# Branch A's key stack in other memory and its first stacks ahead of the last index scores; rotary products and index relu in PSUM

## The reference

```python
def partial_rope(x, cos, sin):
    x1 = xf[..., :half]
    x2 = xf[..., half:ROT_DIM]
    return concatenate([x1 * c - x2 * s, x2 * c + x1 * s, xf[..., ROT_DIM:]], axis=-1)

logits = einsum('bqhd,bsd->bqhs', iqb, ik)
score = einsum('bqhs,bqh->bqs', relu(logits), iwb)
score = where(admissible[None], score, -inf)
_, sel = top_k(score, n_sel)                      # n_sel = 128
s = einsum('bqhgd,bqnhd->bhgqn', qg, k_sel) * scale
p = softmax(s); o = einsum('bhgqn,bqnhd->bqhgd', p, v_sel)
```

## Time and profile before

| | us |
|---|---|
| median of 3 runs | 1347.4 |
| lowest, highest | 1344.56, 1348.52 |
| the profiled execution, whole | 1349.22 |
| its span in the trace | 1347.4 |
| PE busy in it | 1296.7 (96%) |
| DVE, ACT, POOL busy | 721.9 (54%), 622.9 (46%), 617.9 (46%) |
| mean granted TensorE clock | 0.984 of full |

### The profile page before, as it was taken

How to read it: one execution, slowest core, us unless ns; L and a number is a source line. 1 busy time by engine, 2 the same in 40 slices (tenths; PEclk the granted TensorE clock), 3 DMA queues, 4 the chain that set the end, 5 groups by cost and what they waited for, 6 DMA issues and landing times.

```text
span 1347.4 us, 19944 instructions
## 1 busy us (share of the span) xinstructions
PE 1296.7 (96%) x6525; PEld 1087.5 (81%) x6525; DVE 721.9 (54%) x1444; ACT 622.9 (46%) x1119; POOL 617.9 (46%) x767
## 2 busy tenths in 40 slices
PE   5999899999999999999999989999999999999997
PEld 3788788888887888888878868888888878888876
DVE  5688987865446212112658997778545532121154
ACT  4445555776544333323244356576754433233332
POOL 3555433433234545555765543334222445555472
PEclk8999899999999999999999989999999999999998
DMA  5322211221132233233142222112213222332321
GB/s 181 134 92 94 79 63 47 63 87 55 48 110 71 86 101 94 87 105 112 65 175 91 94 81 76 48 55 78 73 48 110 79 71 86 103 99 86 101 94 62
DMA packets 37030, 117.39 MB, mean 87 GB/s; under 512 B 4064, under 2 KB 6496, under 8 KB 36448
## 3 DMA queue, kind: packets, MB, share of 16 engines
q1 hardware_dynamic: 34368, 111.37, 24.9%
q10 hardware_dynamic: 2592, 5.11, 1.3%
HBM read 110.18 MB, written 6.29 MB: 86 GB/s over the span
## 4 chain that ended last, share of the span: by engine, by line
PE 84%; DVE 7%; ACT 4%; issue 2%; POOL 1%; DMA 0%; ACTq 0%; DVEq 0%; SPq 0%; POOLq 0%
PE acc L592 68%; PE ps_o L705 4%; PE ps_t L692 3%; PE ps_s L662 1%; PE ps_t L683 1%; PE ps_o L712 1%; PE ps_s L668 1%; DVE att_c L1311 1%; POOL w_lo L541 1%; PE ps_s L651 1%; DVE ak_s L1152 1%; PE spare L644 1%; DVE score L1179 1%; ACT prob L937 1%; PE ps_s L676 1%
## 5 line engine op out<-in xcount | busy, mean ns | idle before, releaser
L541 POOL TENSOR_TENSOR w_lo<-w_raw,w_hi 128x256 fp32r<-128x256 f32 x752 | 606.5, 837 | 697.2 <-ACT w_hi L787 697.2
L592 PE MATMUL acc<-h_hi,w_hi 128*128 128x512 f32 x1136 | 457.3, 403 | 0.4 <-ACT w_hi L787 0.4
L592 PE MATMUL acc<-h_lo,w_hi 128*128 128x512 f32 x1136 | 448.1, 394 | 0.0
L592 PE MATMUL acc<-h_hi,w_lo 128*128 128x512 f32 x1136 | 297.4, 396 | 2.1 <-POOL w_lo L541 2.1
L787 ACT ACTIVATE w_hi<-w_raw 128x1024 fp32r<-128x1024 f32 (+1 forms) x212 | 203.9, 962 | 130.8 <-PE acc L592 100.6
L592 PEld LDWEIGHTS acc<-h_hi,w_hi 128*128 128x128 f32 x1136 | 215.7, 190 | 41.7 <-ACT w_hi L787 1.3
L592 PEld LDWEIGHTS acc<-h_lo,w_hi 128*128 128x128 f32 x1136 | 215.6, 190 | 40.0
L592 PEld LDWEIGHTS acc<-h_hi,w_lo 128*128 128x128 f32 x1136 | 208.5, 188 | 43.3 <-POOL w_lo L541 3.0
L1324 DVE SCALAR_TENSOR_TENSOR gated<-prob,acc 128x512 f32<-128x512 f32 x16 | 11.0, 687 | 247.6 <-PE acc L592 247.6
L987 ACT ACTIVATE prob<-acc,par_half 128x512 f32<-128x512 f32 x48 | 33.1, 690 | 148.3 <-PE acc L592 148.3
L937 ACT ACTIVATE prob<-prob,neg_max 128x128 f32<-128x128 f32 (+3 forms) x128 | 70.6, 552 | 32.6 <-DVE neg_max L1214 32.0
(11 more groups left out here) (239 smaller groups left out, 1837.1 us busy)
## 6 DMA issues: line engine op xcount, KB each, us to landing
w_raw<-w_full SPq DMA_DIRECT2D x164, 512.0 KB, 3.4
w_raw<-w_mix SPq DMA_DIRECT2D x48, 256.0 KB, 2.6
x_kept<-xT SPq DMA_DIRECT2D x2, 2048.0 KB, 9.4
rel<-rel ACTq DMA_DIRECT2D x16, 256.0 KB, 2.7
xT<-x_kept SPq DMA_DIRECT2D x2, 2048.0 KB, 9.6
stage<-x SPq DMA_DIRECT2D x4, 512.0 KB, 7.0
out<-stage SPq DMA_DIRECT2D x4, 512.0 KB, 2.6
consts<-consts ACTq DMA_DIRECT2D x1, 640.0 KB, 4.2
```

The source lines that it names most:

```text
L541: last = pool.tensor_tensor(w_lo[:, slot, part, :], w_raw[:, raw, part, :], w_hi[:, slot, part, :].bitcast(F32), ALU.subtract)
L592: last = pe.matmul(acc[slot][:, :], w[:, slot, k, :], x[:, k, :], start=(i == 0), stop=(i == 3 * nk - 1))
```

## The change

Four edits.

1. `ak_s` moves from `r0` to the start of `r3`, where branch C's values `cv` will be written much later. The two slots of `aq_s` are swapped: n uses slot (n + 1) % 2, so that n = 0 no longer lies on `ik_s`; the wait for the last index product moves from `ak_hi` to `aq_hi 1`. Branch B's first stacks move by two rows within `r0` to follow the slots.
2. `ak_hi`, `ak_lo` with `aq_hi`, and `aq_lo` of item block 0 go with units 10, 14 and 15. `index (3, h)` goes one unit later (unit 17). `ROUNDS` gives 2 rounds to units 8 to 13 and 4 to units 14 to 16: 24 before the items, 26 in the kernel before. The other two come in the items, so that the mask for t = 3 is written after item 23 instead of item 21.
3. In `rope` the product with the sines goes to PSUM, to the bank `ps_o`, and the last addition reads it there.
4. In `index` ACT writes the relu to PSUM, to `ps_t[h % 2]`, and DVE reads it there.

```diff
-INDEX_AT = {11: 2, 15: 3}
+INDEX_AT = {U_AK + 7: 2, U_AK + 12: 3}
+STACKS_A = {5: ("ak_hi",), 9: ("ak_lo", "aq_hi"), 10: ("aq_lo",)}
-ROUNDS = {8: 2, 9: 2, 10: 2, 11: 2, 12: 2, 13: 4, 14: 4, 15: 4, 16: 4}
+ROUNDS = {U_AK + n: 2 if n < 10 else 4 for n in range(4, 13)}
...
-        if u == 15:
-            seq.extend((("ak_hi", 0), ("aq_hi", 0)))
-        if u == 16:
-            seq.extend((("ak_lo", 0), ("aq_lo", 0)))
+        for step in STACKS_A.get(u - U_AK, ()):
+            seq.append((step, 0))
...
-        ak_s = at("ak_s", [P, 2, 2, SEQ], F32R, r0)
-        bq_s = [at("bq_s0", [P, SEQ], F32R, r0 + 4 * ROW), at("bq_s1", [P, SEQ], F32R, r0)]
+        bq_s = [at("bq_s0", [P, SEQ], F32R, r0 + 6 * ROW), at("bq_s1", [P, SEQ], F32R, r0)]
...
         cv = at("cv", [P, NT, CH, P + 1], F32, r3)
+        ak_s = at("ak_s", [P, 2, 2, SEQ], F32R, r3)
...
-                        act.wait_ge(score_full, l * SCORE_USES + SCORE_USE[("index", (NT - 1, IDX_HEADS - 1))] + 1)
...
                     elif kind == "aq_hi":
                         act.wait_ge(roped, l * ROPES + ROPES)
+                        if n == 1:
+                            act.wait_ge(score_full, l * SCORE_USES + SCORE_USE[("index", (NT - 1, IDX_HEADS - 1))] + 1)
...
-                        act.activation(prob[:, h % 2, 0:(t + 1) * P], ps_s[use % 2][:, 0:(t + 1) * P], ACT.Relu)\
+                        act.activation(ps_t[h % 2][:, 0:(t + 1) * P], ps_s[use % 2][:, 0:(t + 1) * P], ACT.Relu)\
...
-                        link(dve.tensor_tensor(turn[:, :], turn[:, :], sin, ALU.mult))
+                        link(dve.tensor_tensor(ps_o[:, :], turn[:, :], sin, ALU.mult))
                         link(dve.tensor_tensor(t, t, cos, ALU.mult))
-                        dve.tensor_tensor(t, t, turn[:, :], ALU.add).then_inc(roped, 1)
+                        dve.tensor_tensor(t, t, ps_o[:, :], ALU.add).then_inc(roped, 1)
...
-                            dve.tensor_scalar(dst, prob[:, h % 2, 0:w], iw[:, t, h:h + 1], None, ALU.mult).then_inc(score_part, 1)
+                            dve.tensor_scalar(dst, ps_t[h % 2][:, 0:w], iw[:, t, h:h + 1], None, ALU.mult).then_inc(score_part, 1)
```

More of the change, by code:

```diff
@@ L332, in build @@
         sel_f = at("sel_f", [P, CH * P], F32, r6)
-        bq_s = [at("bq_s0", [P, SEQ], F32R, r0 + 4 * ROW), at("bq_s1", [P, SEQ], F32R, r0)]
-        bk_s = [[at("bk_hi_s0", [P, SEQ], F32R, r0 + 5 * ROW), at("bk_lo_s0", [P, SEQ], F32R, r6)],
+        bq_s = [at("bq_s0", [P, SEQ], F32R, r0 + 6 * ROW), at("bq_s1", [P, SEQ], F32R, r0)]
+        bk_s = [[at("bk_hi_s0", [P, SEQ], F32R, r0 + 7 * ROW), at("bk_lo_s0", [P, SEQ], F32R, r6)],
                 [at("bk_hi_s1", [P, SEQ], F32R, r0 + ROW), at("bk_lo_s1", [P, SEQ], F32R, r0 + 2 * ROW)]]
@@ L661, in _ @@
                             for part in range(2):
-                                last = pe.matmul(bank[:, 0:w], aq_s[:, t % 2, h, :], ak_s[:, h // BR, part, 0:w],
+                                last = pe.matmul(bank[:, 0:w], aq_s[:, (t + 1) % 2, h, :], ak_s[:, h // BR, part, 0:w],
                                                  start=(part == 0), stop=(part == 1))
@@ L902, in _ @@
                             g = p // HD * BR
-                            last = act.activation(aq_s[p:p + HD, n % 2, g:g + BR, :], aq[p:p + HD, :, n * P:(n + 1) * P], ACT.Copy)
+                            last = act.activation(aq_s[p:p + HD, (n + 1) % 2, g:g + BR, :], aq[p:p + HD, :, n * P:(n + 1) * P], ACT.Copy)
                         last.then_inc(stack_hi, 1)
@@ L1128, in _ @@
                         if h == 0:
-                            dve.tensor_scalar(dst, prob[:, h % 2, 0:w], iw[:, t, h:h + 1], None, ALU.mult).then_inc(score_part, 1)
+                            dve.tensor_scalar(dst, ps_t[h % 2][:, 0:w], iw[:, t, h:h + 1], None, ALU.mult).then_inc(score_part, 1)
                         else:
-                            dve.scalar_tensor_tensor(dst, prob[:, h % 2, 0:w], iw[:, t, h:h + 1], dst, ALU.mult, ALU.add)\
+                            dve.scalar_tensor_tensor(dst, ps_t[h % 2][:, 0:w], iw[:, t, h:h + 1], dst, ALU.mult, ALU.add)\
                                .then_inc(score_part, 1)
@@ L1158, in _ @@
                             g = p // HD * BR
-                            last = dve.tensor_tensor(aq_s[q:q + HD, n % 2, g:g + BR, :], aq[p:p + HD, :, n * P:(n + 1) * P],
-                                                     aq_s[p:p + HD, n % 2, g:g + BR, :].bitcast(F32), ALU.subtract)
+                            last = dve.tensor_tensor(aq_s[q:q + HD, (n + 1) % 2, g:g + BR, :], aq[p:p + HD, :, n * P:(n + 1) * P],
+                                                     aq_s[p:p + HD, (n + 1) % 2, g:g + BR, :].bitcast(F32), ALU.subtract)
                         last.then_inc(stack_ready, 1)
```

## The result

The kernel after took **1331.1 us** (median of 4 runs, 1330.5 to 1333.3), the kernel before beside it 1347.6 (4 runs, 1344.6 to 1348.5): so 16.5 us less by the medians, where 15.4 were forecast. The ratio, formed from all runs of both, is 0.9885 (15.5 us), 95% interval 0.9868 to 0.9901. The profiled execution of after took 1330.72 us and that of before 1349.22, 18.5 more.

A forecast was written before the change was run, and what follows sets the result against it. PE, busy 96%, bounds the kernel, so only its stalls and lower-clock stretches could give time. Unit 18's 13.1 us plus item 23's 2.3 make 15.4, taking the median 1347.4 to 1332 us (1330.5 to 1334), range 1326 to 1340.

The forecast's parts named there:

- The place at unit 18: Unit 18 to item 3's scores: PE's stall for the query stack shrinks, gaining 6.65 and 6.45 us, 13.1 in all.
- 16.0 at most: Most the reordering could give at unit 18: the 8.1 and 7.9 us lost there in the two layers.
- DVE's readiness at the last sums: DVE reaches the last index sums at 130.9, 0.9 us ahead of their first relu at 131.8.
- Item 23: PE's stalls at item 23 shorten by 0.6 us each and layer 1's clock stays up, 1.1: 2.3 us.
- Covered work: ACT's moved stacks are hidden; 3.0 us of rounds behind item 22 are covered with 1.0 to spare.
- Writing to PSUM: Sine products and relus written to PSUM: no difference; bounds a gain of 0.1 each or a cost of 1.2 a layer.
- Clock lost: Rival: the remaining waits at unit 18 drop the clock, also at layer 1's item 23, losing 3.3: 1335 us; chance 0.10.
- DVE comes earlier: Rival: index sums take 3.0, waits at items 0 and 2 nearly vanish, 1.45 a layer more: 1329 us; chance 0.12.
- Given back: Rival: DVE's 3.0 us added work is uncovered at items 24 to 28, up to 3.0 a layer: 1338 us; chance 0.07.
- the dear PSUM writes: Rival: thirteen PSUM writes ahead of item 0's maximum; at 1.0 us longer each, 1358 us; slower had chance 0.03.
- The change doesn't do what it says: Rival: item 0 would still wait for a stack; held excluded by instruction order, no chance of its own given.

The follow-up runs named there:

- experiment 2: Kernel before with only the rotary product and the relu kept in PSUM; 1348.49 us, ratio 1.0002.
- experiment 5: Kernel after with 26 instead of 24 top-k rounds ahead of the items, tile 3's mask again after item 21; 1342.86 us, ratio 0.9962.
- experiment 4: Kernel after with one PSUM edit undone at a time: rotary products back in SBUF, 1334.65 us; relu back in SBUF, 1332.87 us.
- rotary half of experiment 4: Kernel after with the rotary products back in SBUF, the relu still in PSUM; 1334.65 us, ratio 0.9901.
- experiment 1: Kernel before with only the moved memory and branch A's early stacks, no PSUM edits, 26 rounds, index scores in unit 16; 1344.46 us, ratio 0.996.
- 7: Kernel after with 22 instead of 24 rounds ahead of the items and two rounds with items 9, 12, 15, 16 and 17; 1334.56 us, ratio 0.9905.
- relu half of 4: Kernel after with the relu back in SBUF, the rotary products still in PSUM; 1332.87 us, ratio 0.9891.

## Why the prediction was right, point by point

**The place at unit 18.** Forecast 6.65 + 6.45, with both waits 1.45 a layer; measured 6.32 + 6.15 = 12.5. The waits view counts idle time, 1.02 for the maximum and 0.18 for the exponential; by the starts, as the forecast counted, the pauses are 1.17 and 0.46 (0.85 and 0.6 forecast). The other 0.16 that is missing lies mostly in the first matmul behind each small product, whose successor starts up to 0.32 later and not 0.227. The bound "16.0 at most" held, and the counting of DVE's row gave its end to 0.4 us: item 0's maximum is done at 139.5, on the old axis (unit 18 starts 1.66 later there) 141.1, forecast 140.7. That it came so close is luck in part, as two terms of that row were off and offset each other:

**DVE's readiness at the last sums is the term that was off most.** Forecast 130.9 on the old axis, 0.9 ahead of the relu; in after DVE comes at 130.85 + 1.66 = 132.5, 1.6 later than forecast, and finds the relu ready (ACT's first of two ends at about 130.06; forecast 131.8, which is 130.14 here). DVE's timeline of after, the sums of tile 2 and the last ones:

```profile
101.40 0.62 DVE L1129 TENSOR_SCALAR score<-ps_t,iw 128x384 f32<-128x384 f32 x1 [0.76 <-ACT ps_t L925]
102.32 0.62 DVE L1131 SCALAR_TENSOR_TENSOR score<-ps_t,iw,score 128x384 f32<-128x384 f32 x1 [0.31 <-ACT ps_t L925]
103.37 0.62 DVE L1131 SCALAR_TENSOR_TENSOR score<-ps_t,iw,score 128x384 f32<-128x384 f32 x1 [0.43 <-ACT ps_t L925]
104.42 0.62 DVE L1131 SCALAR_TENSOR_TENSOR score<-ps_t,iw,score 128x384 f32<-128x384 f32 x1 [0.43 <-ACT ps_t L925]
...
130.85 0.75 DVE L1129 TENSOR_SCALAR score<-ps_t,iw 128x512 f32<-128x512 f32 x1
131.64 2.32 DVE L1131 SCALAR_TENSOR_TENSOR score<-ps_t,iw,score 128x512 f32<-128x512 f32 x3
```

The prediction counted 2.1 us from the ropes and 0.5 from tile 2's sums. The additions did become 686 ns each. But four of the five ropes stand ahead of tile 2's sums, and the faster DVE waits there for ACT, 0.76 + 0.31 + 0.43 + 0.43 = 1.93 us, where it did not wait before. Tile 2's sums thus took 4.6 us with their waits, where they had taken 3.7: 0.9 more, not 0.5 less. Another 0.3 is the mask of tile 1, 0.63 now and 0.29 before. It is the effect of experiment 2, one tile earlier; the prediction looked for it at tile 3 and took a gain of 0.5 for tile 2. The other side is at tile 3: DVE came behind the relus and not ahead of them, so it waited for none of the 0.9 that the forecast had it idle, and the sums took 3.3, not 3.6.

**Item 23.** Forecast 0.6 for each stall, measured 0.89 and 0.87; experiment 5 brings both back with two rounds. Forecast 1.1 for the clock behind layer 1's, measured 1.58, since the six small products ran slower too (the matmul behind them starts 1.12 after the first of them, 0.66 in after).

**Covered work.** ACT's stacks and the 3.0 us put behind item 22 cost nothing: PE has no idle before `values` of items 24 to 28, as counted.

**Writing to PSUM.** "No difference", with bounds of a gain of 0.1 and a cost of 0.42 each, was right. The line view of after, by shape (total, mean ns), against the earlier trace rows:

```profile
L1120 DVE TENSOR_TENSOR aq<-aq,ps_o 128x512 f32<-128x512 f32 x8 | 5.5, 686 | 0.3
L925 ACT ACTIVATE ps_t<-ps_s 128x384 f32<-128x384 f32 x8 | 3.8, 475 | 3.2 <-PE ps_s L650 3.2
```

A sine product outside POOL's runs takes 0.70 us where it took 0.69 (starts 90.71 before, 88.63 after), the one inside such a run 1.20 where it took 1.12 (110.42 before, 108.00 after), and the relu of this shape 475 ns where its mean was 488. The Trainium skill (ScalarE: Activation LUTs, "Step-by-step: what each stage is for") says that ScalarE writes faster to PSUM than to SBUF; the traces agree, by 13 ns here.

**The rivals.** "Clock lost" did not come true for waits of 1.02 + 0.18; the clock fell behind 1.71 in one layer of experiment 4, so its margin was under 0.7 us. "DVE comes earlier" fell: the sums took 3.3, but from a later start. "Given back" and the dear PSUM writes did not come true either. "The change doesn't do what it says" fell too: no item waits for a stack.

**Why the total came so close.** By mechanism the change gave 15.8 against 15.4, two misses (0.6 less at unit 18, 1.0 more at item 23) that cancel in part. The medians differ by 16.5, with an interval of 13 to 18, so they can't tell 15.4 from 15.8. The further 1.66 and 0.75 between the profiled executions are the clock of the prologue and of the last transposes, which the forecast had not counted.

## What to carry to other kernels

When an engine waits for a step, count everything the supplier does ahead of the *next* thing it is needed for: moving the step earlier in a full row moves the wait, and only work taken out of the row, or put into a hole in it, shortens it. An edit that makes an engine faster ahead of a place where it waits is worth nothing by itself, and elsewhere no more than what the next wait leaves of it (here 1.2 of 3.1 us a layer), so such edits are judged together, and with each the question is where the engine will next find its input not ready. Before work is pushed later, add up the supplier's idle time up to the next deadline; only so much can go there. And before a difference of a few microseconds is put down to an edit, see in the trace at which instruction it arises: here half of it or more was in some runs the clock, in places that the edit doesn't touch.

## What the runs showed of the hardware

An addition with two SBUF operands took 1110 ns inside POOL's runs; with one of the two in PSUM all sixteen take 686 to 689, the one at 85.16 among them, which lies inside POOL's run from 84.67. The Trainium skill (SBUF — State Buffer, "Terms") describes the port pair that VectorE and GpSimd share as an exclusive lock for which the loser "fully blocks". That the two disturb each other, and that a PSUM operand takes VectorE out of it, the rows bear out. How far one of them blocks the other they don't settle. POOL's run from 86.32 is four instructions; its timeline in the kernel before, cut at the first of them, gives it 1.05 us, where the mean of the line is 0.837:

```profile
86.32 1.05 POOL L541 TENSOR_TENSOR w_lo<-w_raw,w_hi 128x256 fp32r<-128x256 f32 x1 [4.04 <-ACT w_hi L787]
```

The addition begins at 86.81, inside it, and ends at 87.92, 0.55 behind that instruction's end at 87.37, where undisturbed it needs 0.69. So both are lengthened, and most of the addition, but perhaps not all, lies behind POOL's instruction.

The same pause did not always cost the same clock. A wait of 2.85 us kept it in layer 0 and lost it in layer 1 of experiment 5. A wait of 1.71 kept it in layer 0 and lost it in layer 1 of the rotary half of experiment 4. A stall of 1.83 us in layer 1 lost it in the kernel before, in experiments 2 and 5, and kept it in experiment 1, whose PE timeline goes on at full pace:

```profile
855.70 0.85 PE L704 MATMUL ps_o<-av,prob_t 128*128 128x64 f32 x6 [1.83 <-issue]
856.36 0.47 PE L591 MATMUL acc<-h_hi,w_hi 128*128 128x512 f32 x1
856.68 0.39 PE L591 MATMUL acc<-h_lo,w_hi 128*128 128x512 f32 x1
```

The length of the one pause doesn't decide it alone: a pause of 1.65 us before a transpose (`ps_t`, 242 and 885 us in after) kept the clock in both layers of all twelve kernels, and one of 0.88 us, at 307 and 950 us in after, kept it there and lost it once in experiments 1, 7 and the relu half of 4. What a loss cost on top of the pause was 1.1 us behind 0.88, 1.3 to 1.5 behind 1.71, 2.19 and 2.85, and 1.6 behind the stalls of 1.83.

In the prologue the granted clock between 30 and 40 us was 0.69 to 0.71 in the profiled executions of the kernel before, of experiments 1, 2 and 5 and of the rotary half of 4, whose unit 18 starts at 136.4 to 136.6 us; it was 0.83 in after and in the others, where unit 18 starts at 134.7 to 135.9. With one profiled execution of each, whether the kernel decides it or chance stays open, and with it 1 to 2 us of each difference between medians here. Further ahead the view's clock can't be relied on: it gives 1.00 for 20 to 30 us in after, where the timeline has matmuls 0.42 us and more apart until 24.4.

```profile
22.29 0.63 PE L591 MATMUL acc<-xg_lo,w_hi 128*128 128x512 f32 x1
22.71 0.63 PE L591 MATMUL acc<-xg_hi,w_hi 128*128 128x512 f32 x1
```
